# A PE order rewritten in the merged decoding stage: quarters of gate units in slots that had none, thirds of a unit around two halves of a scoring event

## What is computed

```python
h = rms_norm(x, norm_g)
z = einsum('bsd,de->bse', h, w_in)             # q, k, v of both branches, and their gates
qa, ka, va, ga, qb, kb, vb, gb, ma, mb = split(z)
# prompt: 1024 rows; sample: 8 sequences x 8 new tokens, each against 2048 cached positions
o_a = combine_groups(...)                      # dilated windows (128,1), (512,4), (2048,16)
o_b = diff_attention(q, k_all, v_all, ...)     # paged cache, 16 pages of 128 positions a sequence
ya = o_a * silu(ga);  yb = rms_norm(o_b) * silu(gb)
m  = sigmoid(ma) * (ya @ w_proj_a) + sigmoid(mb) * (yb @ w_proj_b)
y  = x + m @ w_out
```

## Time and profile before

| what | value |
|---|---|
| runs | 1696.9, 1701.07, 1702.06 us |
| profiled execution, its own time | 1699.2 us |
| its span (first to last instruction) | 1697.2 us |
| mean granted TensorE clock | 0.992 |
| PE busy | 1631.9 us (96%), 14872 matmuls |
| VectorE, ScalarE, GpSimd busy | 720.7, 598.1, 663.9 us |
| DMA, whole span | 336.30 MB, mean 198 GB/s |

### The profile page before, as it was taken

The page is one execution under the profiler, slowest core; times in us unless marked ns, Lnnn a source line. Parts: engine busy times, 40 slices in busy tenths (PEclk is TensorE's granted clock), DMA queues, the critical chain, the costliest instruction groups (busy, mean ns, idle before and its releaser), DMA issues.

```text
span 1697.2 us, 37775 instructions
## 1 busy us (share of the span) xinstructions
PE 1631.9 (96%) x14872; PEld 1399.5 (82%) x14872; DVE 720.7 (42%) x1788; ACT 598.1 (35%) x1405; POOL 663.9 (39%) x958
## 2 busy tenths in 40 slices
PE   7999999999999999999999989999899999999998
PEld 5787677878899999999999977777777788878787
DVE  6521576222372222722217535335444343588411
ACT  5422477222362222722218234234243334412300
POOL 6566120467433565535656211212221211566500
PEclk9999999999999999999999999999999999999999
DMA  5174810675516568156432879789898987865432
GB/s 169 51 240 148 259 49 13 228 241 189 174 44 212 190 224 275 51 175 218 144 121 70 308 246 335 244 299 347 263 307 297 306 269 237 286 201 178 142 94 81
DMA packets 184064, 336.30 MB, mean 198 GB/s; under 512 B 29969, under 2 KB 74130, under 8 KB 177746
## 3 DMA queue, kind: packets, MB, share of 16 engines
q1 hardware_dynamic: 129762, 196.51, 35.7%
q10 hardware_dynamic: 54128, 137.39, 23.8%
HBM read 294.05 MB, written 127.07 MB: 248 GB/s over the span
## 4 chain that ended last, share of the span: by engine, by line
PE 81%; DMA 6%; SPq 3%; DVE 3%; issue 2%; ACT 2%; POOL 2%; ACTq 1%; POOLq 0%; DVEq 0%
PE ps L2020 14%; PE ps L2022 13%; PE ps L2021 13%; PE ps L2179 4%; PE ps L2077 4%; PE ps L2235 4%; PE ps L2078 4%; PE ps L2079 4%; PE ps L2125 3%; PE ps L2199 3%; PE ps L2294 2%; DMA v_in<-in_cache_a_kv 2%; PE ps L2186 2%; PE ps L2146 2%; PE ps L1989 2%
## 5 line engine op out<-in xcount | busy, mean ns | idle before, releaser
L998 POOL TENSOR_TENSOR w_lo<-raw,w_hi 128x512 fp32r<-128x512 f32 x140 | 180.9, 1298 | 432.2 <-ACT w_hi L1208 431.6
L2020 PE MATMUL ps<-w_hi,hT 128*128 128x512 f32 x824 | 340.4, 413 | 2.3 <-DVE w_lo L1534 1.3
L2022 PE MATMUL ps<-w_hi,hT 128*128 128x512 f32 x824 | 330.4, 401 | 0.0
L2021 PE MATMUL ps<-w_lo,hT 128*128 128x512 f32 x824 | 330.0, 400 | 0.0
L2077 PE MATMUL ps<-w_hi,hT 128*128 128x256 f32 x768 | 223.5, 291 | 1.3 <-issue 1.0
L2020 PEld LDWEIGHTS ps<-w_hi,hT 128*128 128x128 f32 x824 | 206.3, 250 | 22.1 <-DVE w_lo L1534 2.0
L2022 PEld LDWEIGHTS ps<-w_hi,hT 128*128 128x128 f32 x824 | 206.2, 250 | 20.4
L2021 PEld LDWEIGHTS ps<-w_lo,hT 128*128 128x128 f32 x824 | 206.7, 251 | 18.1
L2078 PE MATMUL ps<-w_lo,hT 128*128 128x256 f32 x768 | 216.7, 282 | 2.4 <-issue 2.4
L2079 PE MATMUL ps<-w_hi,hT 128*128 128x256 f32 x768 | 216.3, 282 | 0.0
L1208 ACT ACTIVATE w_hi<-raw 128x512 fp32r<-128x512 f32 x158 | 99.0, 629 | 234.7 <-DMA raw<-in_w_in 197.5
(11 more groups left out here) (233 smaller groups left out, 2848.1 us busy)
## 6 DMA issues: line engine op xcount, KB each, us to landing
out<-in_cache_a_kv ACTq DMA_DIRECT2D x29, 2040.0 KB, 9.3
k_in<-in_cache_b_kv SPq DMA_DIRECT2D x128, 256.0 KB, 4.1
v_in<-in_cache_b_kv SPq DMA_DIRECT2D x128, 256.0 KB, 6.2
raw<-in_w_in SPq DMA_DIRECT2D x104, 256.0 KB, 4.1
k_in<-in_cache_a_kv SPq DMA_DIRECT2D x104, 256.0 KB, 7.6
v_in<-in_cache_a_kv ACTq DMA_DIRECT2D x96, 256.0 KB, 6.8
out<-in_cache_a_kv ACTq DMA_DIRECT2D x7, 2016.0 KB, 8.7
raw<-in_w_in ACTq DMA_DIRECT2D x40, 256.0 KB, 5.4
```

The lines of the kernel that those rows point to most:

```text
L998: pool.tensor_tensor(lo, raw_of(q), hi.bitcast(F32), ALU.subtract).then_inc(lo_done, 1)
L2020: pe.matmul(z, hi, wh, start=first, stop=False)
L2021: pe.matmul(z, hi, wl, start=False, stop=False)
L2022: return pe.matmul(z, lo, wh, start=False, stop=last)
```

## The change

Only the PE's order in the merged stage is changed; no instruction is added or removed.

- `gate(m, first, end)` can now emit any range of a unit's steps (a step is one part k of one row tile: three matmuls, two in a short unit), 16 steps in a full unit, 8 in a short one.
- `scored(x, parts)` can emit two of its four parts j. Its waits stand before the first part, `s_qk` behind the last.
- In a slot with no unit, with a piece, and with exactly one unit in the next slot, the first KC // 2 = 4 steps of that coming unit (a quarter, 12 matmuls; of a short unit half, 8 matmuls) stand between probs and values. Such slots are n = 6 in all eight sequences and n = 2 in six (10, 18, 26, 34, 42, 50).
- In a scoring slot with a full unit what is left of the unit is cut in three: third, first half of the scoring event, third, second half, (summed), third, values. With 16 steps left the thirds are 5, 5 and 6 steps, with 12 left 4, 4 and 4. There are 27 such slots; the slots 15, 21, 35, 41 and 55 have a short unit and keep the event whole and ahead of the unit.

```diff
@@ -2048,21 +2048,21 @@
             def hT_pieces(k, i):
                 return (h[:, k, i * P:(i + 1) * P] for h in hT) if i < NT else (None, None)
 
-            def gate_tiles(m):
-                return range(1 if unit_place(m)[3] == UNITS - 1 else 2)
-
-            def gate(m, tiles=None):
+            def gate_steps(m):
+                return KC if unit_place(m)[3] == UNITS - 1 else 2 * KC
+
+            def gate(m, first=0, end=None):
                 _, _, hb, pr = unit_place(m)
-                tiles = gate_tiles(m) if tiles is None else tiles
-                if 0 in tiles:
+                end = gate_steps(m) if end is None else end
+                if first == 0:
                     if m >= 2:
                         pe.wait_ge(*unit_freed(m - 2))
                     else:
                         pe.wait_ge(ao, 104)
                 z = bank(6 + m % 2)
-                for t in tiles:
+                for t in range(2):
                     i = 2 * pr + t
-                    for k in range(KC):
+                    for k in range(max(0, first - KC * t), min(KC, end - KC * t)):
                         if pr == 0 and t == 0 and (hb == 0 or hb > 1 and k % 2 == 0):
                             pe.wait_ge(*lo_ready(Q_GATE + (KC + NC * (hb - 2) + k // 2 if hb else k)))
                         wh, wl = (half_part(w, hb, k)[:, 0, :] for w in (w_hi, w_lo))
@@ -2077,7 +2077,7 @@
                         pe.matmul(part, hi, wh, start=k == 0, stop=False)
                         pe.matmul(part, hi, wl, start=False, stop=False)
                         ins = pe.matmul(part, lo, wh, start=False, stop=k == KC - 1)
-                if tiles[-1] == gate_tiles(m)[-1]:
+                if end == gate_steps(m):
                     ins.then_inc(z_ready, 1)
 
             def project(br, i):
@@ -2213,28 +2213,31 @@
             def quadrant(c):
                 return slice(ROW_C * c, ROW_C * c + ROWS_S)
 
-            def scored(x):
+            def scored(x, parts=range(4)):
                 b, n = divmod(x, 4)
-                pe.wait_ge(s_kt, tiles_before(2 * x + 2))
-                if x == 0:
-                    pe.wait_ge(as_, 208)
-                if n == 0:
-                    pe.wait_ge(s_qa, b + 1)
-                    if b:
-                        pe.wait_ge(s_tb, b)
-                if n == 2:
-                    pe.wait_ge(s_ta, b + 1)
-                if n == 1:
-                    pe.wait_ge(s_qb, b + 1)
+                if 0 in parts:
+                    pe.wait_ge(s_kt, tiles_before(2 * x + 2))
+                    if x == 0:
+                        pe.wait_ge(as_, 208)
+                    if n == 0:
+                        pe.wait_ge(s_qa, b + 1)
+                        if b:
+                            pe.wait_ge(s_tb, b)
+                    if n == 2:
+                        pe.wait_ge(s_ta, b + 1)
+                    if n == 1:
+                        pe.wait_ge(s_qb, b + 1)
                 for G, at_, tiles in (((3, 0, 8),), ((2, 0, 4),), ((0, 0, 8),), ((0, 0, 8),))[n]:
                     col, at_ = 256 * (n % 2) + 32 * at_, 8 * (x % 2) + at_
-                    for j in range(4):
+                    for j in parts:
                         for c in range(NC):
                             for i in range(4):
                                 rows, d0 = slice(32 * i, 32 * i + 32), c * P + 32 * j
                                 ins = pe.matmul(bank(i)[quadrant(c), col:col + 32 * tiles], q_rep[rows, G, j, c, :],
                                                 k_tiles[rows, at_:at_ + tiles, d0:d0 + 32],
                                                 start=(j == 0 and n in (0, 2)), stop=(j == 3), skip_group_check=True)
+                if parts[-1] < 3:
+                    return
                 if n == 1:
                     for c in range(NC):
                         ins = pe.matmul(bank(1)[quadrant(c), COLS_R:COLS_R + P], q_new[:, 1, c, :],
@@ -2308,21 +2311,33 @@
 
             for m in gates_at(-1):
                 gate(m)
+            begun = 0
             for gg in range(SLOTS):
                 b, n = divmod(gg, 8)
                 mine = pieces_at(gg) if gg < N_GROUPS + 5 else []
                 for pb, p in mine[:1]:
                     probs(pb, p)
-                units = gates_at(gg)
-                parted = gg < N_GROUPS and n % 2 and len(units) == 1 and len(gate_tiles(units[0])) == 2
-                if parted:
-                    gate(units[0], range(0, 1))
+                units, coming = gates_at(gg), gates_at(gg + 1) if gg + 1 < SLOTS else ()
+                at_ = begun
                 if gg < N_GROUPS and n % 2:
-                    scored(gg // 2)
+                    parts = range(4)
+                    if len(units) == 1 and gate_steps(units[0]) == 2 * KC:
+                        gate(units[0], at_, at_ + (2 * KC - at_) // 3)
+                        at_ += (2 * KC - at_) // 3
+                        scored(gg // 2, parts[:2])
+                        parts = parts[2:]
+                        gate(units[0], at_, (at_ + 2 * KC) // 2)
+                        at_ = (at_ + 2 * KC) // 2
+                    scored(gg // 2, parts)
                 if b and n in (1, 5):
                     summed(b - 1, n // 5)
                 for m in units:
-                    gate(m, range(1, 2) if parted else None)
+                    gate(m, at_)
+                    at_ = 0
+                begun = 0
+                if not units and len(coming) == 1 and mine:
+                    begun = KC // 2
+                    gate(coming[0], 0, begun)
                 for pb, p in mine[1:]:
                     probs(pb, p)
                 if n == 2 and b < DEC_B:
```

## The result

The changed kernel takes 1711.5 us (median of 7 runs, 1708.3 to 1716.3) against 1697.3 us (7 runs, 1689.5 to 1702.1) of the kernel before: ratio 1.0093, 95% interval 1.0070 to 1.0115. It is slower by about 14 us. The forecast was 1701.6 us with a range of 1690 to 1711.

A forecast was written before the change was run, and what follows sets the result against it. The PE was taken to set the pace, the DMA not far behind. Savings net of block costs, -11.0 us, and new waits of 5.2, 5.4, 2.1 and 0.7 gave +2.4 on 1699.2: 1701.6 us, range 1690 to 1711.

The forecast's parts named there:

- Terms (a) to (d): Longer waits: ScalarE (n=0 +5.2, n=4 +0.7 us) and value tiles (branch B n=3 +5.4, branch A n=7 +2.1 us).
- L1430's wait: At n = 0, PE comes sooner for ScalarE's copy of piece 3, whose chain is not shorter: +5.2 us (0 to 8.4).
- branch B's: At n = 3, PE waits longer for value tiles queued behind eight key loads: +5.4 us (0 to 7).
- branch A's: At n = 7, slots 15, 31 and 55, PE waits longer for value tiles: +2.1 us.
- the prices of blocks: In 27 slots with halved events, 0.13 us per split plus 0.17 per further gate block: +8.1 us (4.6 to 12.7).
- the savings: Gaps filled -11.2, halved events +8.1, issue idles -7.9 us: -11.0 us before the new waits.
- Quarters in the gaps: In n = 6 and n = 2, quarters fill gaps after transposes: 13.6 us saved, 2.4 for blocks, net -11.2 us.
- half clock: TensorE at 1.2 instead of 2.4 GHz behind long waits; a further fall adds 2 to 3.4 us, only as a rival.
- Issue idles: PE idles awaiting no semaphore at events to be halved, read as instruction supply running dry: -7.9 us (0 to -7.9).
- Rival 2: Chains and DMA landings move along as the cycle shrinks, so fewer new waits: about 1692 us, chance 0.27.
- Rival 3: Instruction supply is not relieved in the split slots, so the 7.9 us are not won: 1709.5 us, chance 0.20.
- Rival 4: The clock falls more often, at slot 48's longer wait or behind grown DMA waits: 1705 to 1709 us, chance 0.11.

The follow-up runs named there:

- change_24: The whole change, quarters and halves kept, but with 24 gate matmuls behind every event: 1699.8 us, ratio 1.0015 to the kernel before.
- halves_only: The changed kernel without quarters, keeping only thirds of a unit around two halves of the event: 1709.2 us, ratio 1.0072 to the kernel before.
- halves_24: Halved events without quarters, ordered 12 matmuls, half, 12, half, 24, so 24 stand behind the event: 1702.8 us, ratio 1.0024 to the kernel before.
- late_sigmoid: The changed kernel, but ScalarE copies probability piece 3 before the sigmoid of slot n = 7's unit: 1707.7 us, ratio 1.0059 to the kernel before.
- quarter_24: Quarters as in the change, every event whole, 24 gate matmuls behind it: 1695.4 us, ratio 0.9979 to the kernel before.
- filled: The changed kernel with extra unread matmuls ahead of the values at its longest waits: 1707.2 us, ratio 1.0067 to the kernel before.

## Why the prediction was wrong

**Right: what gets in the way.** Terms (a) to (d) stood at 13.4 us. change_24 differs from the change in where gate work stands and in 11 gate blocks (2 us), and is 12 us faster; 5 of the 10 us left are the clock's, which these terms did not hold. L1430's wait came out at +6.7 (forecast +5.2), branch B's at +7.2 in one profile and +2.8 in the other (+5.4), branch A's at +1.4 and +3.4 (+2.1). The wait of slot 8 grew by 1.4 us as worked out, that of slot 48 by 2.0. So "the PE comes sooner and the chain is not shorter" is shown by the pairs halves_only and halves_24, change and change_24, and for the copy by late_sigmoid, which shortens the chain instead.

**Right: the prices of blocks.** 1.40 us for a half against 1.38, 0.17 to 0.20 for a gate block: 27 x 0.34 to 0.37 = 9 to 10 us against 8.1.

**The first step that failed: the savings, taken at -11.0 us net.** With the work behind the events left in place they are a loss of 1.3 (medians of change_24 and the kernel before; interval -0.7 to +5.8), though that run has 2 us of blocks fewer and in its one profile still 5.5 us more of waits for tiles than the kernel before. Taken apart:
- *Quarters in the gaps, forecast -11.2.* With the work behind the events unchanged they give -3.1 us (quarter_24, -7.0 to 0). The gaps did close (L1432 from 12.1 to 1.0 us), and the block price was right; but I priced as nothing what comes back when they close: issue idles +4.3, tiles of branch A +3.5, half clock +10 us, worth at most 5 in the profile and 2 over all runs. I had read each gap as lost time; that it was also the time in which the instruction supply and the tile loads caught up fits these numbers and is not shown by a run of its own.
- *Issue idles, forecast -7.9 against blocks of +8.1.* Together they should have cancelled; halves_24 is 4.2 us slower. Its idles fell by 3.3 us, not 6.4, and those of halves_only by 3.4. Halving the events takes 3.3 us of them without quarters and 6.4 with quarters (14.3 us in quarter_24, 7.9 in change_24). The fall by 7.7 in the change itself came only where the waits behind the events had grown as well. The rate that I gave for an event, five times that of a gate block, is six times (256 instructions in 2.63 us against 48 in 2.98).

**The second step: half clock stood in the sum at nothing,** but for 1.5 us that were to be saved. I gave it 2 to 3.4 us for one fall, as a rival, and left it to the range, whose upper end took in only half a fall. The change has four more stretches, worth 6.7 us in its profile and 8 over all runs. That is the largest part of the 12 us by which the forecast change, +2.4, missed the measured, +14.2, and `filled` shows that it counts.

The two accounts see one thing from two sides. In the first profile of the change the gaps and the issue idles did go, 18 to 19 us of listed idle, and longer waits put 18 in their place; in quarter_24 and change_24, where the PE waits less for L1430, issue idles and tile waits came back instead. The PE's idle in the stage is 38.0 us before, 37.3 in the change and 32 to 34 in quarter_24, change_24 and halves_24. What differs beyond that is the price of the blocks and the clock.

**The rivals.** Rival 2 (chains move along) is refuted: the waits came in full. Rival 3 had the time (1709.5) but not the cause: the idles did go, in both profiles of the change. For a kernel with halves alone it was nearer than the forecast, as half of them stayed. Rival 4 had the mechanism, and named slot 48, at too small a price. The rule of the Trainium skill ("Runtime: NRT & Kernel Launch", section "Instruction fetch mechanics") has the fetch hidden in straight code. The idles behind product 117 of slot 7 in two kernels speak against a fetch that is always hidden; that they are fetches is inferred from their place in the stream, no run measured a fetch by itself.

What stays open: how the 8 us between forecast and measured in quarter_24 divide between its three givers-back, since they change from one execution to the next, and what the idles without a releaser are.

## What to carry to other kernels

When work is moved to fill a gap, ask from behind which release it was taken: here 0.7 us of matmuls taken from behind each event's end cost 6 to 8 us, and putting all of them back won 12 of 14, 2 of these by fewer blocks. In a stage that is dense on PE and DMA at once, a filled gap is not all profit (3 of 11 us here). Put the clock into the sum: here the new waits of 2.4 and 4.1 us each had 6.8 us at half clock around or behind them. Before splitting a block of products, price the blocks that come between, not the split.

## What was not expected of the hardware

- Some issue idles are bound to places in the instruction stream. They return behind product 117 of slot 7's event and behind the fourth gate matmul of slot 19 in kernels of different timing, with 0.56 and 2.29, and 2.07 and 0.46 us. Their sum is smaller where events are split and where the PE waits for other things: 2.3 and 3.5 us in the change, 6.6 and 6.7 with halves alone, 10.0 before, 10.4 and 14.3 with quarters alone, 18.4 with a whole event right behind transposes and no wait for L1430.
- On an array split into tiles of 32 rows and 16 columns the end of a block costs little: 32 products take 0.63 us to the next block, 64 take 1.40, 128 take 2.63, so two halves cost 0.17 us more than the whole and four quarters 0.1 less.
- 17 us of matmuls that nobody reads, put into waits, made the kernel 4 us faster.
- The time by which executions of one kernel differ goes with the granted clock, nearly us for us of its at most cost (76 runs).
